# Two encoder layers on one core: the latent stage in a new order, third-attention values by features, its key heads in zero-padded tiles

## The chip, the core and the metric

The kernel runs on one core of a Trainium2 chip. That core has TensorE (PE in the profile, with its weight loads as PEld), VectorE (DVE), ScalarE (ACT), GpSimd (POOL) and the queue of SyncE (SP), which issues the transfers. The metric is the device time of one execution in microseconds (us).

## What is computed

Two layers, each on 512 tokens of 1024 features. The part that matters here is the token mixer: one projected input feeds three attentions, A (causal), C (a window of two chunks of 64 tokens, with 2 key heads for 8 query heads) and B (multi-head latent attention), in that order in the kernel.

```python
h = rms_norm(x, g_mix_pre[i])
z = h @ w_in[i]
aq, ak, av, af, bcq, bckv, bkpe, cq, ck, cv = jnp.split(z, offsets, axis=-1)
...
qf = (rms_norm(bcq, g_mla_q[i]) @ w_mla_uq[i]).reshape(b, s_len, B_HEADS, B_NOPE + B_ROPE)
q_nope, q_pe = qf[..., :B_NOPE], rope(qf[..., B_NOPE:], pos)
kvf = (rms_norm(bckv, g_mla_kv[i]) @ w_mla_ukv[i]).reshape(b, s_len, B_HEADS, B_NOPE + B_V)
k_nope, vbr = kvf[..., :B_NOPE], kvf[..., B_NOPE:]
k_pe = jnp.broadcast_to(rope(bkpe[:, :, None, :], pos), (b, s_len, B_HEADS, B_ROPE))
qb = jnp.concatenate([q_nope, q_pe], axis=-1).transpose(0, 2, 1, 3)
kb = jnp.concatenate([k_nope, k_pe], axis=-1).transpose(0, 2, 1, 3)
yb = blocked_attention(qb, kb, vbr.transpose(0, 2, 1, 3), (B_NOPE + B_ROPE) ** -0.5, False)
yc = banded_sink_attention(cq, ck, cv, sink[i], rel_bias)
...
merged = ga * (ya @ w_branch_a[i]) + gb * (yb @ w_branch_b[i]) + gc * (yc @ w_branch_c[i])
```

## The kernel before

All large products are made of three passes: weights and activations are each split into a high and a low part (`wh`/`wl`, `xnh`/`xnl`, `y0h`/`y0l`, `zkvh`/`zkvl`), and `three()` (L592) multiplies high by high, high by low and low by high. Every engine's program is written out by hand, with semaphores between them. The weights come in chunks of 128x1024 numbers, listed in `CHUNKS`, one list for all engines:

- kf, kA, qA, vA: keys' gates and the A attention's inputs. Then stage A: the chunks qC (4), kC and vC, with the 38 steps of attention A spread between their matmuls.
- Stage C: the 12 chunks gate0 and branch0, with the 38 steps of attention C (the code's attention 1; "third attention" in the title is this one of the reference's C). Its scores are L746, its transposes L756, its products with the values L768.
- The latent stage, between `ST_LAT` and `ST_B`: zq (4 chunks) and zkv (2) make the latents, then uqn (2), uqp, ukn and ukv project them up to B's queries, keys and values. No attention step stands here.
- Stage B: 12 chunks of gate1 and branch1 with the steps of attention B (scores L742), then gate2, branch2, the output product, the channel mixer and the last sub-layer.

For each chunk ScalarE copies the raw weights to `wh` (`hi`, L1007) and VectorE subtracts to make `wl` (`lo`, L1251). There are two pairs of `wh`/`wl`, so that the copy of chunk c+1 waits until TensorE is through with chunk c-1. The results go to two PSUM banks `G` in turn: a tile of results can start when the one two before it has been read out (`g_empty`). Small products (row sums, transposed scales, rotations) go through two banks `AB` in the order of the list `AUX`, in the same manner.

What each engine does in the latent stage before: VectorE scales each latent (L1492), ScalarE squares it (L1017) and makes its high part (L1096), GpSimd adds the squares (L1701, L1703), VectorE makes the low part (L1397). TensorE sums the squares over the features (L604), VectorE takes the inverse root (L1272 to L1277), and TensorE spreads it over the partitions (L620) as `rbq` and `rbkv`. VectorE alone reads out all up-projections: queries (L1403, L1404 and, for the rotary part, L1500), keys (L1403, L1404) and values (L1409); and it does the whole rotation (L1508 to L1524) after the last keys. Then ScalarE copies the shared rotary key to the 8 heads (L1100).

vC before is made by tokens: a weight of 128 columns moves against each of 4 blocks of 128 tokens. A C score takes 64 rows of the array, `kC[r:r + HD]` with `r` 0 or 64:

```python
r, k0 = HD * (h // 4), (0 if i == 0 else P * i - CH)
q, k = qC[r:r + HD, h % 4, P * i:P * i + P], kC[r:r + HD, k0:k0 + nk(i)]
```

## Time and profile before

| what | value |
|---|---|
| median of 3 runs | 2093.56 us (2093.19 to 2094.24) |
| the profiled execution's own time | 2093.33 us |
| its span in the trace | 2091.3 us |
| TensorE busy | 2009.2 us, 96% of the span |
| VectorE, ScalarE, GpSimd busy | 54%, 37%, 6% |
| mean granted TensorE clock | 0.981 of full speed |

The profiled execution lies within the spread of the timed runs, so terms read from the trace can be taken off its own time. TensorE is busy nearly always, but matmuls overlap in the trace, so their starts (one to the next) tell what each costs, and the printed duration does not. One layer's stages in the trace: A from 88 to 181 us, C to 290.9, the latent stage to 384.3, then B. The second layer repeats them some 1038 us later.

### The profile page before, as it was taken

What the parts mean: (1) busy time and instruction counts of PE and PEld (TensorE: products, weight loads), DVE (VectorE), ACT (ScalarE), POOL (GpSimd) and SP (SyncE); (2) the same over time, 40 slices, a digit from 0 to 9 for tenths busy, and PEclk for the clock granted to TensorE, in tenths of its full rate; (3) what the DMA queues carried; (4) which work ended last, traced back from release to release, by engine and by line L of the source; (5) the groups of instructions that cost most, each with busy time, mean ns of one, the idle gap of its engine ahead of it and who ended that gap; (6) DMA issues with size and microseconds to landing.
All of it is one profiled execution on the core that took longest, in us unless ns stands there. A gap on an engine that the chain in (4) does not pass through costs nothing. (4 is left out here: it accounts for less than half of the span.)

```text
span 2091.3 us, 26428 instructions
## 1 busy us (share of the span) xinstructions
PE 2009.2 (96%) x9541; PEld 1622.4 (78%) x9541; DVE 1131.8 (54%) x1983; ACT 783.3 (37%) x1359; POOL 122.6 (6%) x91
## 2 busy tenths in 40 slices
PE   8999998899999999999989999978999999999997
PEld 6777776677878888888867777757788788888886
DVE  5444446544566767525674444464445677774266
ACT  4243431343344444314433434314433344443152
POOL 0000000001100111000000000100001011010000
PEclk9999999899999999999999999989999999999999
DMA  5411132112422333332343111321124233333321
GB/s 156 106 33 41 53 85 75 40 51 61 162 81 84 97 100 93 98 121 91 86 126 81 31 51 51 91 61 51 41 78 154 81 91 100 99 92 111 104 88 71
DMA packets 256436, 176.06 MB, mean 84 GB/s; under 512 B 52148, under 2 KB 240464, under 8 KB 256080
## 3 DMA queue, kind: packets, MB, share of 16 engines
q1 hardware_dynamic: 256200, 174.56, 28.5%
q8 instruction: 63, 1.03, 0.2%
q10 hardware_dynamic: 136, 0.16, 0.1%
q14 instruction: 37, 0.30, 0.0%
HBM read 170.31 MB, written 4.36 MB: 84 GB/s over the span
## 5 line engine op out<-in xcount | busy, mean ns | idle before, releaser
L592 PE MATMUL psum<-xnh,wh 128*128 128x512 f32 (+1 forms) x1408 | 569.0, 404 | 10.0 <-DVE vB L1409 6.3
L592 PE MATMUL psum<-xnh,wl 128*128 128x512 f32 (+1 forms) x1408 | 552.4, 392 | 0.0
L592 PE MATMUL psum<-xnl,wh 128*128 128x512 f32 (+1 forms) x1408 | 551.6, 392 | 0.0
L1251 DVE TENSOR_TENSOR wl<-raw,wh 128x1024 fp32r<-128x1024 f32 (+1 forms) x276 | 364.0, 1319 | 327.2 <-ACT wh L1007 326.6
L1007 ACT ACTIVATE wh<-raw 128x1024 fp32r<-128x1024 f32 (+1 forms) x276 | 291.6, 1056 | 527.0 <-PE psum L592 518.6
L592 PEld LDWEIGHTS psum<-xnh,wh 128*128 128x128 f32 (+1 forms) x1408 | 265.8, 189 | 68.0 <-issue 17.4
L592 PEld LDWEIGHTS psum<-xnh,wl 128*128 128x128 f32 (+1 forms) x1408 | 264.8, 188 | 58.8 <-issue 0.2
L592 PEld LDWEIGHTS psum<-xnl,wh 128*128 128x128 f32 (+1 forms) x1408 | 266.0, 189 | 49.7 <-issue 0.2
L1366 DVE TENSOR_REDUCE mx<-psum 128x1 f32<-128x128 f32 (+3 forms) x128 | 62.6, 489 | 163.0 <-PE psum L743 145.4
L1061 ACT ACTIVATE Pr<-psum,nm 128x128 f32<-128x128 f32 (+3 forms) x128 | 67.7, 529 | 207.4 <-DVE nm L1367 207.4
L592 PE MATMUL psum<-wh,fh 128*128 128x512 f32 x288 | 112.0, 389 | 0.0
L592 PE MATMUL psum<-wh,fl 128*128 128x512 f32 x288 | 112.0, 389 | 0.0
L592 PE MATMUL psum<-wl,fh 128*128 128x512 f32 x288 | 112.0, 389 | 0.0
L1534 DVE TENSOR_TENSOR ub<-psum,rb 128x512 f32<-128x512 f32 x88 | 60.8, 691 | 61.2 <-PE psum L592 60.9
L1724 POOL TENSOR_TENSOR fl<-cv,fh 128x512 f32 x44 | 57.1, 1298 | 542.9 <-ACT fh L1138 542.9
L756 PE MATMUL psum<-cst,Pr 128*128 128x128 f32 x432 | 83.0, 283 | 2.7 <-DVE y0l L1389 2.7
L1073 ACT ACTIVATE PT<-psum 128x256 f32<-128x256 f32 (+3 forms) x192 | 76.5, 399 | 12.1 <-PE psum L756 12.1
L756 PEld LDWEIGHTS psum<-cst,Pr 128*128 128x128 f32 x432 | 47.3, 142 | 38.6 <-issue 26.1
L1138 ACT ACTIVATE fh<-cv 128x512 f32 (+1 forms) x44 | 27.9, 633 | 131.2 <-DVE cv L1553 131.2
L592 PE MATMUL psum<-y0h,wh 128*128 128x512 f32 x176 | 73.4, 417 | 0.0
L1476 DVE TENSOR_TENSOR th<-psum,rb 128x512 f32<-128x512 f32 x48 | 33.1, 689 | 73.0 <-PE psum L592 73.0
L592 PE MATMUL psum<-y0h,wl 128*128 128x512 f32 x176 | 70.7, 402 | 0.0
(235 smaller groups left out, 3023.8 us busy)
## 6 DMA issues: line engine op xcount, KB each, us to landing
raw<-in_w_up_dram SPq DMA_DIRECT2D x88, 512.0 KB, 3.7
raw<-in_w_gate_dram SPq DMA_DIRECT2D x48, 512.0 KB, 3.6
raw<-in_w_down_dram SPq DMA_DIRECT2D x44, 512.0 KB, 3.5
raw<-in_w_in_dram SPq DMA_DIRECT2D x40, 512.0 KB, 3.7
raw<-in_w_out_dram SPq DMA_DIRECT2D x16, 512.0 KB, 3.6
raw<-in_w_ple_gate_dram SPq DMA_DIRECT2D x16, 512.0 KB, 4.3
raw<-in_w_in_dram SPq DMA_DIRECT2D x16, 256.0 KB, 3.3
raw<-in_w_branch_a_dram SPq DMA_DIRECT2D x8, 512.0 KB, 3.3
```

The lines of the kernel that those rows point to most:

```text
L592: ins = pe.matmul(out, left, right, start=start and n == 0, stop=stop and n == 2)
L756: ins = pe.transpose(b[:, P * j:P * j + P], src[:, c0 + P * j:c0 + P * j + P], ident)
L1007: act.activation(halves(c)[0][:, 0:n], raw[s][:, 0:n], ACT.Copy).then_inc(w_hi.sem, 1)
L1061: act.activation(Pr[s % 2][:, c0:c0 + nk], src[:, 0:nk], ACT.Exp, bias=nm[:, i % 2, h:h + 1], scale=scale, accum_out=rsum[:, i % 2, h:h + ...
L1073: act.activation(PT[u % 2][:, 0:w], TBK[tbank[a][("pt", u)]][:, 0:w], ACT.Copy).then_inc(pt_ready.sem, 1)
L1138: act.activation(fh[:, bass.ds(p, 1), :], ft[pair][:, :].rearrange("p (o t) -> p o t", o=1), ACT.Copy).then_inc(f_hi.sem, 1)
L1251: dve.tensor_tensor(low[:, 0:n], raw[(L * NCH + c) % RAW][:, 0:n], hi[:, 0:n].bitcast(F32), ALU.subtract).then_inc(w_lo.sem, 1)
L1366: link(L, dve.tensor_reduce(m, b[:, 0:nk], AX_X, ALU.max))
L1476: dve.tensor_tensor(th[m % 2][:, :], b[:, :], rb[:, :], ALU.mult).then_inc(g_empty.sem, 1)
L1534: dve.tensor_tensor(u[:, 2:T + 2], G[g % 2][:, :], rb[:, :], ALU.mult).then_inc(g_empty.sem, 1)
L1724: pool.tensor_tensor(fl[:, bass.ds(p, 1), :], ft[j][:, :].rearrange("p (o t) -> p o t", o=1), fh[:, bass.ds(p, 1), :].bitcast(F32), ALU.su ...
```

## The change

- The latent stage's up-projections stand in the order uqp, uqn, uqn, ukv, ukn (before: uqn, uqn, uqp, ukn, ukv).
- The queries' inverse root is no longer spread over the partitions nor multiplied into the queries. It is kept by token (`rq`, `nrq`) and goes into the softmax of attention B, as the scale of the exponential and the factor of the maximum. ScalarE reads out the queries and the values with plain copies; VectorE keeps the keys.
- The rotation of the queries is done after uqn instead of after ukn, by VectorE in place, and ScalarE copies its result to the heads in 8 instructions. The shared key's rotation and its copy to 8 heads move up to the middle of the latents.
- VectorE adds the squares, GpSimd none. The row sums of the query latents (L604 before, L610 after) are taken after zkv 1, those of the key latents after the first uqn.
- vC comes before kC and is made by features like all others (24 matmuls of 512 columns); four transposes after kC's product turn it by tokens, and one copy puts it in place.
- kC has two tiles `kC[0]` and `kC[1]` of 128 rows, each with one head's 64 rows and zeros in the others; a score takes all 128 rows of `qC`.

The diff's pieces below are, in order: the lists, SyncE's load of the rotary table, TensorE's C score, its transposes of vC, its latent stage, ScalarE's latent stage, the softmax of attention B, VectorE's read-outs of vC and kC, and its latent stage.

```diff
-    + [("qC", m) for m in range(4)] + [("kC", 0), ("vC", 0)]
+    + [("qC", m) for m in range(4)] + [("vC", 0), ("kC", 0)]
...
-CHUNKS += [("uqn", 0), ("uqn", 1), ("uqp", 0), ("ukn", 0), ("ukv", 0)]
+CHUNKS += [("uqp", 0), ("uqn", 0), ("uqn", 1), ("ukv", 0), ("ukn", 0)]
...
-AUX = ["rb0", "vec", "csq", "rbq", "cskv", "rbkv", "rot0", "rot1", "rotk", "rb2", "pt0", "pt1"]
+AUX = ["rb0", "vec", "rotk", "csq", "cskv", "rot0", "rot1", "rbkv", "rb2", "pt0", "pt1"]
...
-                if c == ST_LAT + 5:
+                if c == ST_LAT + 4:
                     wait(y_lo.sem, y_lo.at(L, 2 * TB))
...
-                    r, k0 = HD * (h // 4), (0 if i == 0 else P * i - CH)
-                    q, k = qC[r:r + HD, h % 4, P * i:P * i + P], kC[r:r + HD, k0:k0 + nk(i)]
+                    k0 = 0 if i == 0 else P * i - CH
+                    q, k = qC[:, h % 4, P * i:P * i + P], kC[h // 4][:, k0:k0 + nk(i)]
...
+                if kind == "kC":
+                    pe.wait_ge(g_empty.sem, g_empty.at(L, G_BASE[c]))
+                    o = g_open(1)
+                    for t in range(TB):
+                        ins = pe.transpose(o[:, P * t:P * t + P], th[0][:, P * t:P * t + P], ident)
+                    ins.then_inc(vt_full.sem, 1)
...
+            slot(L, ST_LAT)
+            slot(L, ST_LAT + 1)
+            b = aux_open(L, "rotk")
+            pe.matmul(b[:, :], rot[0:ROPE, :], kf[0:ROPE, :], start=True, stop=True).then_inc(aux_full.sem, 1)
+            for c in range(ST_LAT + 2, ST_LAT + 8):
+                slot(L, c, beside=lambda k, c=c: c == ST_LAT + 5 and k == KT - 1 and z_sums(L, "q"))
+            z_sums(L, "kv")
+            turn_half(L, 0)
+            slot(L, ST_LAT + 8, beside=lambda k: turn_half(L, 1))
+            slot(L, ST_LAT + 9, beside=lambda k: spread_scale(L, "kv"))
+            slot(L, ST_LAT + 10)
...
-            for c in range(ST_LAT, ST_B):
+            for c in range(ST_LAT, ST_LAT + 6):
                 slot(L, c)
+            shared_key(L)
+            hi(L, ST_LAT + 7)
+            post(L, ST_LAT + 5)
+            queries_out(L, ST_LAT + 6, 0)
+            for c in (ST_LAT + 7, ST_LAT + 8):
+                queries_out(L, c - 1, 1)
+                hi(L, c + 1)
+                queries_out(L, c, 0)
+            queries_out(L, ST_LAT + 8, 1)
+            hi(L, ST_LAT + 10)
+            act.wait_ge(g_empty.sem, g_empty.at(L, G_BASE[ST_B - 2]))
+            for t in range(TB):
+                values_out(L, ST_B - 2, t)
+            hi(L, ST_B)
+            for j in range(2):
+                turned_queries(L, j)
...
-                scale = BSCALE if a == 2 else 1.0
+                scale = rq[:, i:i + 1] if a == 2 else 1.0
...
-                dve.tensor_scalar(neg, m, -BSCALE if a == 2 else -1.0, None, ALU.mult).then_inc(max_done.sem, 1)
+                dve.tensor_scalar(neg, m, nrq[:, i:i + 1] if a == 2 else -1.0, None, ALU.mult
+                                  ).then_inc(max_done.sem, 1)
...
+                elif kind == "vC":
+                    dve.tensor_tensor(th[0][:, :], b[:, :], rb[:, :], ALU.mult).then_inc(g_empty.sem, 1)
+                    for g in range(2):
+                        dve.memset(kC[g][HD - HD * g:P - HD * g, :], 0.0)
...
+            elif kind == "kC":
+                dve.wait_ge(w_used.sem, w_used.at(L, c + 1))
+                for g in range(2):
+                    own = slice(HD * g, HD * g + HD)
+                    ins = dve.tensor_tensor(kC[g][own, :], G[G_BASE[c] % 2][own, :], rb[own, :], ALU.mult)
+                ins.then_inc(g_empty.sem, 1)
+                dve.wait_ge(vt_full.sem, vt_full.at(L, 1))
+                dve.tensor_copy(vC[:, :, :].rearrange("p t e -> p (t e)"), G[(G_BASE[c] + 1) % 2]
+                                ).then_inc(g_empty.sem, 1)
...
                 j = c - ST_LAT - 2
-                if 0 <= j < 6 and j != 5:
+                if 0 <= j < 6:
                     latent_lo(L, j)
-                if j == 3:
+                    add_squares(L, j)
+                if j == 2:
+                    shared_key(L)
+                if j == 4:
                     row_scales(L, "q")
-                if j == 4:
-                    latent_lo(L, 5)
-                    scale_rows(L, "q", rbq)
+                if j == 6:
                     row_scales(L, "kv")
-                if j == 5:
-                    scale_rows(L, "kv", rbkv)
+                    rope(L, 0)
+                    rope(L, 1)
```

What stands in each engine's row, at three places. First ScalarE in the latent stage of layer 0, from the read-out of the second-last latent on, before the change. L1007 is the copy of a weight chunk, L1017 a square, L1096 a latent's high part.

```order
L1007 ACTIVATE wh<-raw 128x1024 [waits w_landed2,w_used]
L1017 ACTIVATE sq_82<-Sp_72 128x512 [waits sq_used,g_empty]
L1096 ACTIVATE zkvh<-Sp_72,vec 128x512
L1007 ACTIVATE wh<-raw 128x1024 [waits w_landed3,w_used]
L1007 ACTIVATE wh<-raw 128x1024 [waits w_landed0,w_used]
L1007 ACTIVATE wh<-raw 128x1024 [waits w_landed1,w_used]
L1007 ACTIVATE wh<-raw 128x1024 [waits w_landed2,w_used]
L1100 ACTIVATE kB<-ytok 32x4096 [waits kpe_ready]
L1007 ACTIVATE wh<-raw 128x1024 [waits w_landed3,w_used]
```

And the same engine and place of the changed kernel (L1012 is the copy of a weight chunk there, L1019 a square, L1100 a high part):

```order
L1148 ACTIVATE kB<-ytok 32x4096 [waits kpe_ready]
L1012 ACTIVATE wh<-raw 128x1024 [waits w_landed2,w_used]
L1019 ACTIVATE sq_82<-Sp_72 128x512 [waits sq_added,g_empty]
L1100 ACTIVATE zkvh<-Sp_72,vec 128x512
L1133 ACTIVATE Pr_73<-psum 128x512 [waits t_full,g_full]
L1133 ACTIVATE Pr_74<-psum 128x512 [waits t_full,w_used]
L1012 ACTIVATE wh<-raw 128x1024 [waits w_landed3,w_used]
L1136 ACTIVATE qB<-psum 64x512 [waits g_full]
L1137 ACTIVATE qB<-psum 64x512
...
L1142 ACTIVATE vB<-psum,rcol 128x512 [waits rcol_ready,w_used]
L1012 ACTIVATE wh<-raw 128x1024 [waits w_landed2,w_used]
L1155 ACTIVATE qB<-Pr_73 32x512 [waits rope_sum]
```

The copy of the shared key (32x4096) stands ahead of the weight chunks of the up-projections instead of behind them, and the read-outs of queries, values and rotated queries stand between the weight copies.

Second, VectorE at the end of the latent stage, before the change (keys' third and fourth tile, the rotation, the first values):

```order
L1403 TENSOR_TENSOR kB<-psum,rbkv 64x512 [waits w_used]
L1404 TENSOR_TENSOR kB<-psum,rbkv 64x512
L1508 TENSOR_TENSOR Pr_73<-Sp_71,trig 128x512 [waits trig_in]
L1511 TENSOR_TENSOR PT_75<-psum,trig 128x512 [waits aux_full]
L1514 TENSOR_TENSOR qB<-Pr_73,PT_75 32x512 [waits aux_empty]
L1514 TENSOR_TENSOR qB<-Pr_73,PT_75 32x512 x3
L1508 TENSOR_TENSOR Pr_74<-Sp_72,trig 128x512
L1511 TENSOR_TENSOR PT_76<-psum,trig 128x512 [waits aux_full]
L1514 TENSOR_TENSOR qB<-Pr_74,PT_76 32x512 [waits aux_empty]
L1514 TENSOR_TENSOR qB<-Pr_74,PT_76 32x512 x3
L1518 TENSOR_TENSOR th_77<-kf,trig 32x512
L1521 TENSOR_TENSOR th_78<-psum,trig 32x512 [waits aux_full]
```

And after it (L1305 is the low part of a weight chunk there, L1472 and L1473 the keys):

```order
L1573 TENSOR_TENSOR Pr_74<-Pr_74,PT_76 128x512 [waits aux_empty,dve_link]
L1305 TENSOR_TENSOR wl<-raw,wh 128x1024 [waits w_hi]
L1363 COPY rbkv<-psum 128x512 [waits aux_full]
L1472 TENSOR_TENSOR kB<-psum,rbkv 64x512 [waits g_full,g_empty,aux_empty]
L1473 TENSOR_TENSOR kB<-psum,rbkv 64x512
L1472 TENSOR_TENSOR kB<-psum,rbkv 64x512 [waits g_full]
L1473 TENSOR_TENSOR kB<-psum,rbkv 64x512
L1305 TENSOR_TENSOR wl<-raw,wh 128x1024 [waits w_hi]
L1472 TENSOR_TENSOR kB<-psum,rbkv 64x512 [waits g_full]
L1473 TENSOR_TENSOR kB<-psum,rbkv 64x512
L1472 TENSOR_TENSOR kB<-psum,rbkv 64x512 [waits w_used]
L1473 TENSOR_TENSOR kB<-psum,rbkv 64x512
```

The rotation is gone from behind the keys; the keys are the stage's last read-out, with the low part of gate1's first chunk between the second and the third tile.

Third, TensorE at the border of stages A and C in the changed kernel (L791 are the last transposes of attention A, L838 the four of vC, L760 the first score of attention C):

```order
L791 MATMUL psum<-cst,ytok 128x128 x3
L598 MATMUL psum<-xnh,wh 128x512
L598 MATMUL psum<-xnl,wh 128x512
L598 MATMUL psum<-xnh,wl 128x512
L598 MATMUL psum<-xnh,wh 128x512
L598 MATMUL psum<-xnl,wh 128x512
L598 MATMUL psum<-xnh,wl 128x512
L838 MATMUL psum<-cst,th_77 128x128 [waits g_empty]
L838 MATMUL psum<-cst,th_77 128x128 x3
L598 MATMUL psum<-xnh,wh 128x512 [waits g_empty,w_lo,w_hi]
L598 MATMUL psum<-xnl,wh 128x512
L598 MATMUL psum<-xnh,wl 128x512
```

Before, 24 matmuls of vC (128x128, with no attention among them) stood between those last transposes and the first chunk of stage C, and that chunk's bank had been read out long before; now six matmuls of kC and the four transposes stand there, and the first chunk of stage C waits (`g_empty`) for the read-out of kC's tile.

## Rows read from the trace of the kernel before

**Rows 1.** Page, part 1: busy time, share of the span, instructions.

```profile
PE 2009.2 (96%) x9541; PEld 1622.4 (78%) x9541; DVE 1131.8 (54%) x1983; ACT 783.3 (37%) x1359; POOL 122.6 (6%) x91
```

**Rows 2.** Waits of PE: for what, us in total, times, longest.

```profile
PE psum L592 <- DVE vB L1409: 11.9, 4, 3.2
...
PE psum L924 <- DVE PT L1511: 10.0, 2, 5.0
PE psum L592 <- DVE Sp L1500: 6.4, 2, 3.2
PE psum L604 <- POOL acc L1701: 6.4, 2, 3.2
```

**Rows 3.** Windows: length, busy us of each engine, granted clock, DMA share, GB/s.

```profile
290.85:384.30 93.45, 76.17 (x296) 58.92 (x294) 57.29 (x88) 23.15 (x25) 7.06 (x4) 0.88 0.27 68
384.30:390.10 5.80, 5.80 (x17) 4.71 (x18) 1.24 (x5) 0.46 (x2) 0.00 (x0) 0.50 0.27 90
```

**Rows 4.** Timeline of PE, latent stage of layer 0: start, us, instruction.

```profile
290.85 0.39 PE L592 MATMUL psum<-xnh,wh 128*128 128x512 f32 x1
...
317.82 0.39 PE L592 MATMUL psum<-xnh,wl 128*128 128x512 f32 x1
318.05 0.95 PE L604 MATMUL psum<-cst,acc 128*128 128x1 f32 x8
...
360.14 1.88 PE L922 MATMUL psum<-Sp,cst 128*128 128x512 f32 x4
367.00 2.07 PE L924 MATMUL psum<-kf,cst 32*128 32x512 f32 x2 [4.98 <-DVE PT L1511]
...
384.29 0.76 PE L592 MATMUL psum<-xnh,wh 128*128 128x512 f32 x1 [3.16 <-DVE vB L1409]
```

**Rows 5.** Timeline of PE, chunk vC of layer 0, a stretch without attention.

```profile
175.07 0.28 PE L592 MATMUL psum<-wl,xnh 128*128 128x128 f32 x1
...
177.75 0.28 PE L592 MATMUL psum<-wl,xnh 128*128 128x128 f32 x1
```

**Rows 6.** Timeline of PE around an A score (65 rows), then a C score (64).

```profile
94.69 0.40 PE L592 MATMUL psum<-xnh,wl 128*128 128x512 f32 x1
94.92 0.38 PE L742 MATMUL psum<-kA,qA 65*128 65x128 f32 x2
95.15 0.22 PE L743 MATMUL psum<-cbf 128*128 128x128 bf16 x1
...
236.03 0.39 PE L592 MATMUL psum<-xnh,wl 128*128 128x512 f32 x1
236.35 0.59 PE L746 MATMUL psum<-kC,qC 64*128 64x192 f32 x2
236.87 0.44 PE L756 MATMUL psum<-cst,Pr 128*128 128x128 f32 x2
```

**Rows 7.** Timelines of ACT and DVE, last tile of attention A.

```profile
178.52 0.60 ACT L1079 ACTIVATE y0h<-psum 128x512 fp32r<-128x512 f32 x1 [6.90 <-PE psum L777]
179.15 0.69 DVE L1389 TENSOR_TENSOR y0l<-psum,y0h 128x512 fp32r<-128x512 f32 x1 [4.19 <-ACT y0h L1079]
```

**Rows 8.** Groups by form, whole trace: busy us, mean ns, idle before.

```profile
L1007 ACT ACTIVATE wh<-raw 128x1024 fp32r<-128x1024 f32 x274 | 290.6, 1061 | 523.6 <-PE psum L592 518.6 <-DMA raw<-in_w_up_dram 2.4 <-DMA raw<-in_w_ple_dram 1.9
...
L1117 ACT ACTIVATE pl<-psum 128x512 f32<-128x512 f32 x16 | 9.3, 596 | 7.9 <-PE psum L592 7.8
...
L1100 ACT ACTIVATE kB<-ytok 32x4096 f32<-32x4096 f32 x2 | 7.2, 3615 | 29.1 <-DVE ytok L1524 29.1
...
L1251 DVE TENSOR_TENSOR wl<-raw,wh 128x1024 fp32r<-128x1024 f32 x274 | 363.0, 1325 | 325.1 <-ACT wh L1007 324.5
...
L1397 DVE SCALAR_TENSOR_TENSOR y0l<-Sp,vec,y0h 128x512 fp32r<-128x512 f32 x8 | 12.1, 1518 | 0.0
...
L1403 DVE TENSOR_TENSOR kB<-psum,rbkv 64x512 f32<-64x512 f32 x8 | 5.5, 683 | 5.5 <-PE psum L592 5.3
...
L1701 POOL TENSOR_TENSOR acc<-sq,sq 128x512 f32<-128x512 f32 x4 | 6.9, 1727 | 586.6 <-ACT sq L1017 586.6
```

More of the change, by code:

```diff
@@ L106 @@
 WIDTH = {"kf": KT * 40}
-G_OF = {"vA": 0, "out": 0, "down": 0, "pg": 0, "vC": 2, "uqn": 2, "uqp": 2, "ukn": 4, "ukv": 4, "ple": TB,
+G_OF = {"vA": 0, "out": 0, "down": 0, "pg": 0, "kC": 2, "uqn": 2, "uqp": 2, "ukn": 4, "ukv": 4, "ple": TB,
         "branch0": 2, "branch1": 2, "branch2": 2}
@@ L338, in trunk_kernel @@
     trig = here("trig", 48, [P, 2, T])
-    rbq = here("rbq", 52, [P, T])
     rbkv = here("rbkv", 54, [P, T])
@@ L829, in slot @@
                             ins.then_inc(wide_full.sem, 1)
-            elif kind == "vC":
-                for j in range(2):
-                    o = g_open(j)
-                    for t in range(2):
-                        tb = 2 * j + t
-                        for k in range(KT):
-                            ins = three(o[:, P * t:P * t + P], c, P * k, P, xnh[:, k, P * tb:P * tb + P],
-                                        xnl[:, k, P * tb:P * tb + P], k == 0, k == KT - 1, w_moves=True)
-                            if t == 1 and k == KT - 1:
-                                ins.then_inc((w_used if j == 1 else g_full).sem, 1)
-                            if k % 4 == 3:
-                                between(4 * j + 2 * t + k // 4)
             elif kind[:6] == "branch":
@@ L858, in slot @@
                     ins.then_inc((w_used if j == 1 else g_full).sem, 1)
+                    if j == 0 and beside is not None:
+                        beside(0)
             elif kind == "ukn":
@@ L872, in slot @@
                     ins.then_inc((w_used if t == TB - 1 else g_full).sem, 1)
+                    if t == 1 and beside is not None:
+                        beside(0)
             elif kind == "ple":
@@ L1118, in ple_out, with taken_bank, queries_out, values_out @@
                                ).then_inc(g_empty.sem, 1)
+        def taken_bank(L, c, j):
+            if j == G_OF[CHUNKS[c][0]] - 1:
+                act.wait_ge(w_used.sem, w_used.at(L, c + 1))
+            else:
+                act.wait_ge(g_full.sem, g_full.at(L, GP_BASE[c] + j + 1))
+            return G[(G_BASE[c] + j) % 2]
+        def queries_out(L, c, j):
+            kind, m = CHUNKS[c]
+            b = taken_bank(L, c, j)
+            if kind == "uqp":
+                act.wait_ge(t_full.sem, t_full.at(L, 2 * STEPS))
+                act.activation(Pr[j][:, :], b, ACT.Copy).then_inc(g_empty.sem, 1)
+            else:
+                h = 4 * m + 2 * j
+                act.activation(qB[0:HD, h, :], b[0:HD, :], ACT.Copy)
+                act.activation(qB[0:HD, h + 1, :], b[HD:P, :], ACT.Copy).then_inc(g_empty.sem, 1)
+        def values_out(L, c, t):
+            b = taken_bank(L, c, t)
+            act.wait_ge(rcol_ready.sem, rcol_ready.at(L, RB_NORMS.index("kv") + 1))
+            act.activation(vB[:, t, :], b, ACT.Copy, scale=rcol[:, t:t + 1]).then_inc(g_empty.sem, 1)
+        def shared_key(L):
+            if L > 0:
+                act.wait_ge(x_spilled.sem, 16 * L)
+            act.wait_ge(kpe_ready.sem, kpe_ready.at(L, 1))
+            act.activation(kB[NOPE:NOPE + ROPE, :, :],
+                           ytok[0:ROPE, :].rearrange("p (o t) -> p o t", o=1).to_broadcast([ROPE, H, T]),
+                           ACT.Copy).then_inc(kpe_placed.sem, 1)
+        def turned_queries(L, j):
+            act.wait_ge(rope_sum.sem, rope_sum.at(L, j + 1))
+            for q in range(4):
+                ins = act.activation(qB[NOPE:NOPE + ROPE, 4 * j + q, :], Pr[j][32 * q:32 * q + 32, :], ACT.Copy)
+            ins.then_inc(rope_ready.sem, 1)
         def up_post(L, s, it):
@@ L1399, in latent_lo, with add_squares @@
                                      ).then_inc(z_lo.sem, 1)
+        def add_squares(L, j):
+            if j in (0, 4):
+                return
+            dve.wait_ge(sq_ready.sem, sq_ready.at(L, j + 1))
+            if j in (2, 3):
+                dve.wait_ge(sq_added.sem, sq_added.at(L, j - 1))
+            out, one = (sq[0], sq[0]) if j == 5 else (acc, sq[0] if j == 1 else acc)
+            dve.tensor_tensor(out[:, :], one[:, :], sq[j % 2][:, :], ALU.add).then_inc(sq_added.sem, 1)
         def heads_apart(L, b, dst, j, scale):
@@ L1463, in post @@
                                       ).then_inc(wide_empty.sem, 1)
[L1464 to L1470 removed]
+            elif kind == "kC":
[7 more added lines that the diff above has]
+                                ).then_inc(g_empty.sem, 1)
             elif kind[:4] == "gate":
                 br = int(kind[4])
+                if br == 1 and m == 0:
+                    dve.wait_ge(g_empty.sem, g_empty.at(L, G_BASE[c]))
                 if br == 2 or (br == 1 and m >= 2):
@@ L1557, in slot @@
             last = CHUNKS[c - 1][0] if c else None
-            late = last not in ("ukn", "ukv") and kind not in ("ukn", "ukv")
-            if not late:
-                lo(L, c + 1)
             if last == "ukn":
```

183 lines of the change are left out of this document (65 added, 118 removed).

## Prediction

> **What bounds the kernel now.** First the busy shares: TensorE is busy 2009.2 of 2091.3 us, VectorE 54%, ScalarE 37% [rows 1]. So time can come from TensorE's own work or from its few waits, from nothing else. Next TensorE's waits: the four longest groups, 11.9, 10.0, 6.4 and 6.4 us, all fall in the latent stage [rows 2], the same ones in each layer, 34.7 us together or 17.3 a layer. In three the one waited for is VectorE's read-out or rotation, in the fourth GpSimd's addition. The windows then show a second price of these waits: over the 93.45 us of layer 0's latent stage the granted clock is 0.88 of full, and in the 5.80 us behind its last wait it is 0.50, which is 1.2 instead of 2.4 GHz [rows 3]. Since a share of 1 - 0.88 lost means twice that share at the lower level, some 22 us of the stage ran there.
>
> **Latent stage, what can be had.** At the full clock 119 steps from matmul to matmul take 317.82 - 290.85 = 26.97 us, 0.2266 each [rows 4]. The stage has 11 chunks of 24: 264 x 0.2266 = 59.8 us. Its small products: two row sums at 0.8 (318.05 to the next start, close to the printed 0.95), four rotation matmuls in 1.7 to 1.9, the shared key's, 2.07 at the low clock, so 1.0 to 1.1, two spreads of some 0.35, and about 0.1 at each of nine returns to the large products: 6 us [rows 4]; the last two figures are estimates. So 66 us of work stand in a stage of 384.29 - 290.85 = 93.4 [rows 4]: 27.4 us are waits and low clock. Behind it 5.8 us at half clock hold 2.7 us more [rows 3]. At most 30 us a layer.
>
> **What the new order leaves of it.** I count from the first zq as 0, with 5.44 us a chunk. The changed rows put uqp at 34.6, uqn at 40 and 47 to 54, ukv at 54 to 59 and ukn last. ScalarE's queue is the one to follow, as a late weight copy stops TensorE. A weight copy costs 1.06, a read-out of 128x512 0.6, the shared key's copy 3.62 [rows 8]. Zkv 0 is squared and copied by 31; the key's copy, now ahead of everything, runs 31 to 34.7; the copy for the first uqn ends at 35.8, VectorE's low part (1.33 [rows 8]) at 37.1, needed at 40. Behind it queue the second zkv's square (added on VectorE at 44.5, wanted at 45.5 by the row sum, the thinnest margin) and the read-outs of uqp (38.1, 40.8). Each later chunk costs ScalarE 1.06 + four half read-outs of 0.6 = 3.5 of 5.44 us. It fits: low parts are done at 43, 49 and 57, wanted at 47, 54 and 59.5. The values wait for rcol, ready at 52. The rotation is on VectorE from 51.7 to 56, while TensorE runs uqn and ukv, so the 4.98 us wait of the shared key's matmul [rows 4] has nothing left to wait for: that matmul moved to where `kf` is long ready. Removing `rbq` takes a spread (0.35) and VectorE's copy away. In the queue of SyncE the rotary table moves one weight chunk up, behind a wait for attention C's last low part; that falls near the start of zq 0, and the next weight load cannot go before zq 1's low part anyway: nothing.
>
> What is late next are keys. Two read-outs of 64 rows, 0.68 each [rows 8], serve one tile that TensorE makes in 6 x 0.2266 = 1.36: VectorE only just keeps up, it begins when the last values are out (60.4), and the low part of gate1's chunk stands between tile 2 and tile 3. I get a wait of 0.3 in ukv, 0.35 before ukn's third tile and 1.25 before gate1, whose bank is ukn's third: 1.9 a layer. Whether a wait as short as 1.3 us drops the clock is open; a drop cost 2.7 us behind the stage's last wait of 3.2 [rows 3, 4], and I take a third of that, 0.8. Latent stage: 27.4 + 2.7 + 0.35 - 1.9 - 0.8 = **27.7 us a layer**.
>
> On VectorE four additions of 0.7 are new, but its low parts of the latents took 1.52 us in the mean [rows 8], and ran beside GpSimd's additions of 1.73 [rows 8]. The Trainium skill, VectorE: DVE Perf Modes, writes of the second SBUF read interface as shared with GpSimd; by that the low parts fall back to about the 0.7 of a read-out and pay for the additions. By the sum above VectorE had room either way.
>
> **vC by features.** 24 matmuls of 128x128 take 177.75 - 175.07 = 2.68 us, 0.112 each [rows 5]; 96 are 10.7 us. After: 24 x 0.2266 = 5.4, four transposes 0.45 (as 128x128 matmuls), and about 0.05 more at each of some eight switches between attention and 512 columns, 0.4. **4.4 us a layer**, all on TensorE's path. The attention steps are the same and have waited for nothing there.
>
> **Padded key heads.** An A score (65 rows, so no half of the array) begins 94.92 - 94.69 = 0.23 behind the last product, and the next instruction begins 0.23 behind it, for 128 columns in two passes; 192 columns are 0.34. A C score (64 rows, 192 columns) begins 0.32 behind and lasts 0.52 to the next start [rows 6]. So 0.84 against 0.57: 0.27 for each; with 128 columns likewise. 32 scores a layer: **8.8 us a layer**. The Trainium skill, TensorEngine Tiling (Array Packing), Key Properties, says that a change of tiling mode drains TensorE, and here the gap ahead of the 64-row score agrees. The same section speaks against the padding too: 64-row tiles work independently, two scores at once. By the drain the sum is 17.6 us for both layers, by lost overlap it would be nothing. In [rows 6] each 64-row score stands alone among 128-row products, so no overlap is there to lose; the streamed columns are the same.
>
> **Border of stages A and C.** New here: the last transposes of attention A stand 6 matmuls before kC's end. ScalarE's copy begins 178.52 and VectorE's low part 179.15 to 179.84 [rows 7], some 2.0 us behind the transposes; counted from kC's end, at +0.2 or so. Only then come kC's two read-outs, 2 x 0.68, and gate0 waits for them: +1.75, against +0.46 when TensorE is through with vC's transposes. A wait of 1.3 us, plus 0.4 for the smaller chance of a low clock: **-1.7 us a layer**. The copy of vC (0.7) and the 3 first matmuls of gate0 (0.7) then run side by side.
>
> Sum: 27.7 + 4.4 + 8.8 - 1.7 = 39.2 a layer, **78.4 us**. The profiled execution's own time of 2093.33 is 0.2 below the median, so both give 2093.3 - 78.4 = **2015 us**.
>
> **Bounds.** Below: no new wait, no low clock, 45 a layer: 2003. The unmeasured things: the scores' saving, 0.20 to 0.33 each (13 to 21 us); ScalarE's half read-outs from PSUM, 0.6 by the nearest row, at most 1.06, that of twice the columns [rows 8]; the exponential with a scale per token, which by its neighbours costs nothing or up to 0.1 for 64 steps, hidden; and the low clock, 0 to 5.4 us a layer. With all of them bad at once the gain is still 78 - 5 - 9 - 8 = 56, that is 2037.
>
> **Rivals.**
> 1. ScalarE's queue is late in the latent stage. For it: 32x4096 (3.62) now blocks weight copies, and the row sum of the keys has 1 us of margin. Against: ScalarE was busy 23.15 of 93.45 us there [rows 3], and 22 added copies of 0.6 make 36 of 66. If each of three or four chunks waits 1.5 us and the clock falls each time, 10 us a layer are given back: 2035. Chance 0.13.
> 2. Padding does nothing, the gap belongs to fp32 behind the split products. Against: the A score has no such gap [rows 6]. 2033. Chance 0.05.
> 3. It is slower. One mechanism: the read-outs on ScalarE. The latent stage has 22 new ScalarE instructions a layer, each between a weight copy and the bank TensorE waits for. They cost 0.6; if they cost 1.8 us more each, all in TensorE's way, 39.6 us a layer are gone and the time is 2094; from there on it is slower, at 2.5 more each it is 2125. Only the 3.62 of the 4096-column copy is of that size, and it has eight times the columns. Chance 0.04, a quarter of it within 0.2% of no change.
> 4. The order takes the waits away, but short ones keep the clock low: two more drops a layer of 2.7 us, 2026. Chance 0.14, inside the range.
> The forecast itself: 0.64.
>
> A measurement of this kernel can tell 0.2%, 4 us. All cases but the third are faster: faster 0.96, same 0.01, slower 0.03. Range: from 2005, near the bound, to 2037, past rivals 1 and 2.
>
> **What the profile will show.** TensorE's waits in the latent stage 1 to 3 us a layer, none on a rotation, none on GpSimd; the stage some 67 us long at a granted clock near 1. C scores 0.23 behind their predecessor and 0.34 to the next. vC's chunk with 512 columns, a wait near 1.3 at gate0's first matmul with VectorE's kC as releaser, and one like it at gate1. Wrong would be: waits for ScalarE's copies (`wh`, `qB`, `vB`) of over 5 us a layer, or a granted clock under 0.95 there.

## The result, and the profile after

The changed kernel takes 2011.32 us in the median of 4 runs (2010.56 to 2016.67) against 2093.38 of the kernel before beside it: the ratio is 0.9615, 95% interval 0.9601 to 0.9629, faster by 82.1 us (by the interval 78 to 84). The forecast was 2015 (2005 to 2037). The profiled execution took 2011.93, its span is 2010.1 us. One execution of e2_vc below took 2144.42 us at a granted clock of 0.898 and is left out of its median.

First the busy shares of the changed kernel, page part 1, which answer to [rows 1]:

```profile
span 2010.1 us, 26179 instructions
PE 1954.9 (97%) x9397; PEld 1599.2 (80%) x9397; DVE 1106.0 (55%) x1955; ACT 815.2 (41%) x1403; POOL 107.6 (5%) x83
```

ScalarE has taken work over (783.3 us before), and VectorE is busy 26 us less: its read-outs went, and the squares' additions that came are small. Waits of TensorE (for whom, us in total, times, the longest), against [rows 2]; the first, for `xt`, is outside of all that was changed:

```profile
PE psum L644 <- DVE xt L1394: 11.4, 4, 4.4
...
PE psum L770 <- DVE y0l L1448: 2.7, 2, 1.4
PE psum L598 <- DVE kB L1473: 2.7, 4, 1.1
PE psum L598 <- DVE kC L1535: 2.3, 2, 1.1
```

The four groups of the latent stage, 34.7 us, are gone; `kB` and `kC` (2.7 and 2.3 us in both layers) are the forecast's new waits at gate1 and gate0, and nothing of the rotation or of GpSimd is left. Windows of the changed kernel: from the first zq to B's first score in layer 0, the 5.80 us behind it, stages A and C of layer 0, then stage C and the latent stage of layer 1 (length in us, busy us of each engine, granted clock, DMA share, GB/s), against [rows 3]:

```profile
277.02:345.12 68.10, 66.77 (x295) 52.96 (x293) 40.11 (x72) 36.55 (x47) 0.00 (x0) 1.00 0.35 87
345.12:350.92 5.80, 5.80 (x32) 4.90 (x31) 3.20 (x8) 1.56 (x8) 0.00 (x0) 1.00 0.47 140
89.07:177.08 88.01, 84.00 (x500) 66.75 (x501) 39.39 (x93) 39.76 (x108) 0.00 (x0) 1.00 0.13 37
177.08:277.02 99.94, 97.34 (x534) 82.51 (x534) 49.54 (x147) 43.15 (x123) 0.00 (x0) 1.00 0.23 65
1174.50:1274.41 99.91, 97.38 (x534) 82.41 (x534) 49.61 (x147) 43.11 (x123) 0.00 (x0) 1.00 0.23 65
1274.41:1342.51 68.10, 66.77 (x294) 52.95 (x293) 40.12 (x72) 36.56 (x47) 0.00 (x0) 1.00 0.36 88
```

The granted clock of the stage was 0.88 before and is 1.00 now; in the stretch behind it it went from 0.50 to 1.00. From the first zq to B's first score it is 68.10 us in both layers, 94.85 and 94.58 before. Between the same marks (the first scores of A, C and B, the first zq, the first matmul of the output product) the two traces give, layer 0 and layer 1:

| stretch | before | after | gain |
|---|---|---|---|
| A score to C score | 92.89, 91.25 | 88.01, 88.06 | 4.9, 3.2 |
| C score to zq | 109.03, 109.04 | 99.94, 99.91 | 9.1, 9.1 |
| zq to B score | 94.85, 94.58 | 68.10, 68.10 | 26.8, 26.5 |
| B score to output product | 183.58, 183.40 | 182.10, 182.09 | 1.5, 1.3 |

They sum to 82.3; with 1.1 lost elsewhere, nearly all behind the last output product, that is 81.2, the difference of the spans. The 1.6 by which layer 0's first row exceeds layer 1's is a stretch of low clock that, of these two executions, only the one of the kernel before has there. It comes and goes (see the fourth experiment), so it is no gain of the change.

At the border of A and C, timeline of PE of the changed kernel (start, duration, instruction, wait); the C scores answer to the 64-row score in [rows 6]:

```profile
176.31 0.47 PE L598 MATMUL psum<-xnh,wh 128*128 128x512 f32 x1 [1.14 <-DVE kC L1535]
176.62 0.39 PE L598 MATMUL psum<-xnl,wh 128*128 128x512 f32 x1
176.85 0.40 PE L598 MATMUL psum<-xnh,wl 128*128 128x512 f32 x1
177.08 0.39 PE L760 MATMUL psum<-kC,qC 128*128 128x128 f32 x2
177.22 0.48 PE L598 MATMUL psum<-xnh,wh 128*128 128x512 f32 x1
```

A score begins 0.23 behind its predecessor, where it was 0.32 to 0.35. Over all 64 scores of each trace, from the start of the predecessor to the start of what follows the score, it was 0.84 to 0.85 with 192 columns and 0.75 with 128, and is 0.55 and 0.45 now: 0.3 less for a score, 0.1 ahead of it and 0.2 behind. The heads in rows 0 to 63 and those in rows 64 to 127 were alike before. Groups by form of the changed kernel, the copies that went to ScalarE and two that stayed (busy us, mean ns, idle before), against [rows 8]:

```profile
L1148 ACT ACTIVATE kB<-ytok 32x4096 f32<-32x4096 f32 x2 | 7.3, 3628 | 0.0
...
L1456 DVE SCALAR_TENSOR_TENSOR y0l<-Sp,vec,y0h 128x512 fp32r<-128x512 f32 x8 | 6.0, 746 | 0.0
...
L1142 ACT ACTIVATE vB<-psum,rcol 128x512 f32<-128x512 f32 x8 | 5.5, 689 | 3.8 <-PE psum L598 3.6
...
L1137 ACT ACTIVATE qB<-psum 64x512 f32<-64x512 f32 x8 | 4.8, 595 | 0.1
L1136 ACT ACTIVATE qB<-psum 64x512 f32<-64x512 f32 x8 | 4.7, 592 | 15.0 <-PE psum L598 15.0
```

The half read-outs cost the 0.6 that was taken for them. The low parts of the latents fell from the 1518 ns of [rows 8] to 746 (why: fourth experiment).

### The profile page after: what moved, and what is told of

The parts are those of the page before. It is cut to its first block, busy times and chain, and to the rows that moved or that the text cites. A ratio compares the mean times of both kernels' runs of the same rounds, so it can differ in the third digit from the quotient of the medians.

```text
span 2010.1 us, 26179 instructions
## 1 busy us (share of the span) xinstructions
PE 1954.9 (97%) x9397; PEld 1599.2 (80%) x9397; DVE 1106.0 (55%) x1955; ACT 815.2 (41%) x1403; POOL 107.6 (5%) x83
## 4 chain that ended last, share of the span: by engine, by line
PE 88%; DVE 6%; issue 3%; ACT 3%; DMA 0%; SPq 0%; DVEq 0%; ACTq 0%
PE psum L598 76%; PE psum L782 4%; PE psum L756 3%; PE psum L770 2%; ACT wh L1012 1%; PE psum L760 1%; DVE xt L1394 1%; PE psum L644 1%; DVE mx L1424 1%; PE psum L791 1%; DVE yg_down L1386 0%; DVE oP L1375 0%; ACT Pr L1065 0%; ACT PT L1077 0%; DVE xnl L1319 0%
## 5 line engine op out<-in xcount | busy, mean ns | idle before, releaser
L1305 DVE TENSOR_TENSOR wl<-raw,wh 128x1024 fp32r<-128x1024 f32 (+1 forms) x276 | 364.4, 1320 | 318.6 <-ACT wh L1012 318.0
L1012 ACT ACTIVATE wh<-raw 128x1024 fp32r<-128x1024 f32 (+1 forms) x276 | 291.2, 1055 | 452.8 <-PE psum L598 444.7
L1754 POOL TENSOR_TENSOR merged<-merged,th 128x512 f32<-128x512 f32 x32 | 43.1, 1351 | 976.1 <-DVE th L1556 975.8
L1065 ACT ACTIVATE Pr<-psum,nm,rq 128x128 f32<-128x128 f32 (+3 forms) x64 | 39.6, 619 | 108.9 <-DVE nm L1425 108.9
L1176 ACT ACTIVATE fh<-cv 128x512 f32 (+1 forms) x44 | 27.8, 632 | 131.3 <-DVE cv L1613 131.3
L770 PEld LDWEIGHTS psum<-cst,Pr 128*128 128x128 f32 x432 | 51.0, 142 | 27.7 <-issue 15.3
```

Source lines behind the costliest of these rows:

```text
L770: ins = pe.transpose(b[:, P * j:P * j + P], src[:, c0 + P * j:c0 + P * j + P], ident)
L1012: act.activation(halves(c)[0][:, 0:n], raw[s][:, 0:n], ACT.Copy).then_inc(w_hi.sem, 1)
L1065: act.activation(Pr[s % 2][:, c0:c0 + nk], src[:, 0:nk], ACT.Exp, bias=nm[:, i % 2, h:h + 1], scale=scale, accum_out=rsum[:, i % 2, h:h + ...
L1305: dve.tensor_tensor(low[:, 0:n], raw[(L * NCH + c) % RAW][:, 0:n], hi[:, 0:n].bitcast(F32), ALU.subtract).then_inc(w_lo.sem, 1)
L1754: pool.tensor_tensor(merged[:, m, :], merged[:, m, :], th[m % 2][:, :], ALU.add).then_inc(m_added.sem, 1)
```

## Experiments: the parts by themselves

The code cuts below are shortened: they show what changes, not every line. Four kernels ran on one chip beside the kernel before, which took 2091.69 there.

**e1_pad**, the kernel before with the padded heads alone (the score is shown; kC's two fills and two read-outs come with it):

```diff
-r, k0 = HD * (h // 4), (0 if i == 0 else P * i - CH)
-q, k = qC[r:r + HD, h % 4, P * i:P * i + P], kC[r:r + HD, k0:k0 + nk(i)]
+k0 = 0 if i == 0 else P * i - CH
+q, k = qC[:, h % 4, P * i:P * i + P], kC[h // 4][:, k0:k0 + nk(i)]
```

> The kernel before with one part of the change: the key heads of attention C in two zero-padded tiles of 128 rows. Theory (a 64-row score among 128-row products makes TensorE stop and start again): each of the 64 scores gains 0.27 to 0.29 us, so 17 to 18.5 us, 2075 to 2076; the score starts 0.23 behind the product before it. Rival (the gap belongs to fp32 products behind the split ones, whatever their rows): no gain, 2093. VectorE's two fills and second read-out, 1.7 us a layer, lie beside products of vC and cost nothing under either.

Measured: 2072.71, ratio 0.9915 (0.9903 to 0.9928), -19.0 us. Stage C from its first score to zq fell from 109.03 (what TensorE was busy in it: 107.15) to the first line here; the second is the same stage of the kernel with vC alone. Windows:

```profile
180.10:280.60 100.50, 97.50 (x534) 82.61 (x534) 49.71 (x147) 43.52 (x124) 0.00 (x0) 1.00 0.22 64
```
```profile
178.40:287.43 109.03, 107.15 (x535) 79.22 (x535) 49.37 (x147) 43.14 (x123) 0.00 (x0) 1.00 0.20 58
```

At the same number of matmuls and the same clock it is 8.5 us a layer less, 0.27 for each of 32 scores. That is net of new waits: the third score starts 0.77 behind its predecessor, 0.37 of it idle for the first exponential, and TensorE waits three times 0.16 for ScalarE's `PT`. By the starts, as above, a score with half of the rows between products with all of them costs 0.3 more, though it streams the same columns.

**e2_vc**, the kernel before with vC by features ahead of kC, transposed behind it (the lists and the read-out; one `kC` as before):

```diff
-[("kC", 0), ("vC", 0)]
+[("vC", 0), ("kC", 0)]
+ins = pe.transpose(o[:, P * t:P * t + P], th[0][:, P * t:P * t + P], ident)
```

> The kernel before with one part of the change: vC by features, kC last, with kC in one tile of 64-row heads as before. Theory: 4.4 us a layer less of TensorE's work, less a wait for kC's read-out at gate0 of about 0.5 (one read-out of 0.69 instead of two), so 3.9 a layer, 2085.5. Rival (the added wait also drops the clock, 2.7 us each time): 2088 to 2091.

Measured: 2081.34, ratio 0.9951 (0.9938 to 0.9964), -10.4. In its trace the stretch from A score to C score is 89.03 and 89.07, in both layers with one stretch of low clock of 1.6: without it 3.8 a layer less than before, 7.6 in all, which lies at the lower end of the interval. With one read-out of kC the wait at gate0 is 0.4, and no low clock stands behind it: the rival did not come.

**e3_latent**, the changed kernel with vC and the key heads as before (the diff's pieces on `vC`, `kC` and the C score undone):

> The changed kernel with vC by tokens and the key heads of attention C in one tile, as before, so that only the latent stage and the softmax scale of attention B differ from before. Theory: 27.7 us a layer by the forecast's sum, 2038; TensorE waits 1 to 2 us a layer there and its clock is full. Rival (part of the gain comes from elsewhere, such as an earlier start of attention B's steps or fewer low-clock stretches at other places): 2045 or more.

Measured: 2039.44, ratio 0.975 (0.9737 to 0.9762), -52.3; zq to B score is 68.10, what the changed kernel has. The forecast's 27.7 a layer would be 55.4. In the trace the last two stretches of the table give 56.0, and 2.8 are lost from the output products on, where one low stretch is 3.4 us longer than in the trace before. So the three parts give 19.0 + 10.4 + 52.3 = 81.7 by themselves and 82.1 together: within the 3 us that each interval allows, they do not overlap.

**e4_pool_squares**, the changed kernel with the squares added by GpSimd, at the moved places:

```diff
-add_squares(L, j)   # VectorE, behind each latent's low part
+for j in (1, 2, 3, 5):   # GpSimd
+    add_squares(L, j)
```

> The changed kernel with the squares of the latents added on GpSimd again, all else as changed. Theory (it is the later place of the row sums that took the wait away, not the engine): GpSimd's four additions of 1.7 us end before the sums are asked for, except the last, wanted 1 us after VectorE's was ready, so at most 1 us of wait a layer: 2011 to 2014. Rival (the engine made the wait): 3.2 us of wait and 2.7 of low clock a layer come back, 2023.

Measured: 2014.19, ratio 0.9627 (0.9615 to 0.964). TensorE waits for no row sum, and zq to B score is 68.10 and 68.11: the later place is enough to take the wait away, whichever engine adds. Two groups of its trace, then VectorE and GpSimd at one latent:

```profile
L1456 DVE SCALAR_TENSOR_TENSOR y0l<-Sp,vec,y0h 128x512 fp32r<-128x512 f32 x8 | 12.2, 1520 | 0.0
L1745 POOL TENSOR_TENSOR acc<-acc,sq 128x512 f32<-128x512 f32 x4 | 7.2, 1808 | 17.1 <-ACT sq L1019 17.1
```
```profile
303.32 1.23 DVE L1305 TENSOR_TENSOR wl<-raw,wh 128x1024 fp32r<-128x1024 f32 x1 [0.34 <-ACT wh L1012]
303.88 1.81 POOL L1745 TENSOR_TENSOR acc<-acc,sq 128x512 f32<-128x512 f32 x1 [3.63 <-ACT sq L1019]
304.47 1.77 DVE L1456 SCALAR_TENSOR_TENSOR y0l<-Sp,vec,y0h 128x512 fp32r<-128x512 f32 x1
```

The mean of 1520 ns mixes two values, here as in [rows 8]: the low parts with an addition beside them take 1.77 to 1.78 us, those with none 0.75. So the low part and the addition together cost VectorE less by itself (some 1.4 us) than the low part alone does beside GpSimd. The low part shown ends 0.55 behind the addition that was running when it began. The Trainium skill, VectorE: DVE Perf Modes, Two Vector instructions with no wait between them, was drawn on for this in the prediction (a read interface shared with GpSimd); the trace agrees, 1.78 against 0.75 us, now by switching it.

Its median lies 2.9 us above the changed kernel's, its profiled execution (2016.48) 4.6, and none of it is in the latent stage. Of the 4.6, 3.2 are low clock in stage A of both layers: a window of e4_pool_squares, and the same of the changed kernel:

```profile
117.10:120.50 3.40, 3.40 (x14) 2.75 (x13) 0.58 (x2) 0.75 (x4) 0.00 (x0) 0.50 0.33 98
```
```profile
117.10:120.50 3.40, 3.40 (x19) 2.62 (x18) 0.58 (x2) 0.96 (x4) 0.00 (x0) 1.00 0.24 71
```

Both stand behind the same wait, which every kernel of this study has once a layer; here it is in the changed one:

```profile
115.83 0.44 PE L770 MATMUL psum<-cst,Pr 128*128 128x128 f32 x2 [1.38 <-DVE y0l L1448]
```

In the 14 profiled executions of this study the wait was 1.37 or 1.38 us 28 times, and 12 times a 3.4 us stretch at half clock stood behind it, which costs 1.6. That is up to 3.2 us of the 2 to 6 us by which each kernel's runs differ. The other runs have no trace, but their time goes with the clock: of the changed kernel's four, the fastest (2010.56) was granted 0.995 and the slowest (2016.67) 0.992. This makes a gain of 2 us hard to see below.

## Experiments: who is the bound, and what a wait costs

Four kernels on a second chip (the kernel before: 2091.35), then four on a third (2093.09).

**e5_dve_queries**, uqn's read-outs back on VectorE:

```diff
-act.activation(qB[0:HD, h, :], b[0:HD, :], ACT.Copy)   # and the other half
+dve.tensor_copy(qB[0:HD, h, :], b[0:HD, :])   # and the other half, in VectorE's row
```

> The changed kernel, with one thing back: the eight 64-row read-outs of uqn's queries a layer are VectorE's again, as plain copies, instead of ScalarE's (uqp's and the values' stay with ScalarE). Theory, the order made the gain and VectorE has room: a chunk of uqn costs VectorE 1.33 for its low part and 4 x 0.68 for the read-outs, 4.05 of the 5.44 us that TensorE takes, so the time is that of the changed kernel within 0.2%, 2009 to 2016 us, with at most a few tenths of new wait in the latent stage. Rival, the relief of VectorE made it: its queue (latents' low parts, squares, rotation, rbkv, keys) is late by some 5.4 us a layer at the end of the stage, the rotation and the keys come late, waits of 2 to 5 us a layer appear with low clock behind them: 2018 to 2030 us.

Measured: 2023.36, ratio 0.9668 (0.9654 to 0.9681). My theory fell, and the rival's size is right: some 12 us, though its waits for keys and rotation did not come. The timeline of PE:

```profile
332.90 0.39 PE L598 MATMUL psum<-y0h,wl 128*128 128x512 f32 x1
335.37 0.70 PE L598 MATMUL psum<-wh,zkvh 128*128 128x512 f32 x1 [2.08 <-DVE qB L1569]
```

and of DVE, before that wait ends:

```profile
327.73 0.16 DVE L1341 TENSOR_SCALAR rtmp<-psum 128x4 f32<-128x4 f32 x1
...
329.99 0.68 DVE L1576 TENSOR_TENSOR PT<-psum,trig 128x512 f32<-128x512 f32 x1
...
333.23 0.69 DVE L1579 TENSOR_TENSOR Pr<-Pr,PT 128x512 f32<-128x512 f32 x1
333.84 0.68 DVE L1568 COPY qB<-psum 64x512 f32<-64x512 f32 x1
```

The inverse root of the keys' scale and the rotation, 6.1 us together, stand ahead of the second chunk's read-outs. zq to B score is 71.81 in both layers, 3.7 more: 2.08 of wait and 1.6 of low clock behind it. That makes 7.4 in both layers; its profiled execution has stage A's low clock in both as well, 3.2.

**e10_late_rotation**, the same with the rotation behind those read-outs:

```diff
-if j == 6: row_scales(L, "kv"); rope(L, 0); rope(L, 1)
+if j == 6: row_scales(L, "kv")
+if j == 7: rope(L, 0); rope(L, 1)
```

> As the run with uqn's read-outs on VectorE, but with the rotation of the queries one chunk later there, behind the read-outs of the second uqn chunk. Theory, what cost 7 us was the place and not the load: the row scales and the rotation (6 us) stood ahead of two read-outs for which TensorE waited 2.1 us a layer, with low clock behind; with them out of the way the waits for qB go and the time is that of the changed kernel or up to 2 us more, 2010 to 2014. Rival, VectorE has too much work there whatever its order: a wait of 1 us or more a layer comes back at the keys or at ukv (for the rotated queries or rbkv), and it stays at 2018 to 2023.

Measured: 2015.42, ratio 0.9636 (0.9622 to 0.9649). Of the wait for `qB` 0.12 is left, and zq to B score is 68.70. The 0.6 more than in the changed kernel are 0.2 at the values' tile behind that wait and 0.4 at `rbkv`'s spread, which waits 0.20 for the rotation. The profiled execution took 2012.98, inside what was expected; the median is 1.4 above that and 3.1 above the changed kernel's on the same chip, where the two intervals still overlap. So VectorE can carry these read-outs at 0.6 us a layer, and e5 lost its time by their place; putting them on ScalarE only spared the change from having to place them well.

**e6_gap3** and **e7_gap6**, the changed kernel with a longer wait ahead of gate0 (n = 3 and 6):

```diff
 elif kind == "kC":
     dve.wait_ge(w_used.sem, w_used.at(L, c + 1))
+    for _ in range(n):
+        link(L, dve.memset(vC[:, :, :], 0.0))
```

> The changed kernel with three more fills of vC with zeros on VectorE, each waiting for the one before, ahead of kC's read-outs (nothing that is computed changes). They lengthen TensorE's wait ahead of gate0 from 1.1 to about 2.7 us. Theory, a wait of this length drops the clock (all waits of 2.7 us and more did in the kernel before, those of 1.1 never did in the changed one): 1.6 of wait and about half of a 3.4 us stretch at half clock, 1.7, a layer, 6 to 7 us in all: 2017 to 2019. Rival, the clock falls only with longer waits: 3 us, 2014 to 2015, and no stretch below full clock behind gate0's start.

> As the one before with six fills, so that TensorE waits about 4.3 us ahead of gate0. Theory: the wait is 3.2 us a layer longer than in the changed kernel and the stretch at half clock costs 1.7 or, as behind the waits of 3.2 to 6 us in the kernel before, 2.7 to 3.4: 10 to 13 us in all, 2021 to 2025. Rival, a drop doesn't depend on this wait: 6.4 us, 2018.

Measured: 2020.56 and 2026.45, ratios 0.9668 and 0.9687, against 2011.80 of e8_pool_lo on the same chip, which ties with the changed kernel (next experiment). The waits were longer than meant, one PE line of each:

```profile
178.68 0.77 PE L598 MATMUL psum<-xnh,wh 128*128 128x512 f32 x1 [3.11 <-DVE kC L1537]
```
```profile
1185.95 0.76 PE L598 MATMUL psum<-xnh,wh 128*128 128x512 f32 x1 [5.09 <-DVE kC L1537]
```

and a stretch of low clock came with each of the four. Windows of e6 in layer 0, then of e7 in layer 1:

```profile
177.70:184.50 6.80, 5.82 (x16) 4.80 (x17) 4.96 (x14) 0.52 (x3) 0.00 (x0) 0.50 0.24 77
```
```profile
1183.00:1189.80 6.80, 3.85 (x10) 3.20 (x11) 5.76 (x12) 0.00 (x0) 0.00 (x0) 0.50 0.11 24
```

From A score to zq, with the added wait (1.97 and 3.95) and any low clock of stage A taken off, the stretch cost 2.56 and 1.41 in e6 (6.8 and 3.4 us long) and 1.42 and 1.57 in e7 (3.4 and 6.8). In these four cases a wait that is 2 us longer does not cost more in low clock: of e7's 6.8 us, 2.95 ran off while TensorE still waited. The theory that the drop comes with these waits holds; that it would grow with the wait does not. From one fill to the next it took 0.66 us instead of the 0.53 assumed, so both times lie above what was expected: 3.9 + 4.0 for e6 and 7.9 + 3.0 for e7 by these sums, against the measured 8.8 and 14.7; of the latter 1.6 is stage A's low clock in the profiled execution, and some 2.3 lie far from the wait: 0.85 ahead of A's first score, 0.5 and 0.95 behind the two output products.

**e8_pool_lo** and **e11_pool_lo_again**, gate1's first low part on GpSimd:

```diff
+if c == ST_B:
+    dve.wait_ge(w_lo.sem, w_lo.at(L, ST_B + 1))
+if c + 1 != ST_B:
     lo(L, c + 1)
# GpSimd makes that low part
+pool.tensor_tensor(wl, raw, wh, ALU.subtract).then_inc(w_lo.sem, 1)
```

> The changed kernel, but the low part of gate1's first weight chunk is made by GpSimd instead of VectorE, where it stands between the keys' second and third tile. Theory, this low part (1.33 us on VectorE) is what TensorE's wait of 1.1 us ahead of gate1 comes from: the wait goes, 1.1 to 1.4 us a layer, 2009 us, if GpSimd's 128x1024 subtraction (twice the 1.73 us of its 128x512 additions, some 3.5) is done before TensorE wants it about 5 us after the copy. Rival, GpSimd takes longer than that or slows VectorE's key read-outs beside it: a wait of 1 to 3 us for GpSimd in its place, 2011 to 2018.

> The changed kernel once more, to stand beside the three others on one chip. 2009 to 2013 us; a stretch at half clock in stage A, behind the 1.38 us wait for y0l, may stand in one layer or none, 1.6 us each.

> The run with gate1's first low part on GpSimd once more, beside the changed kernel on one chip. Theory: its stage is 0.97 us a layer shorter as before, and it is 2 us faster than the changed kernel in the median; what hid this was low clock in stage A of its profiled execution, which comes and goes. Rival: the low clock is moved and not removed, and the two times agree within 0.5 us.

Measured: 2011.80, ratio 0.9622 (0.9609 to 0.9635); on the third chip 2012.07 (0.962, 0.9605 to 0.9634) beside 2012.34 of the changed kernel itself (e9_changed_again: 0.9624, 0.9609 to 0.9639; there the change is worth 80.8 us). GpSimd's subtraction:

```profile
L1756 POOL TENSOR_TENSOR wl<-raw,wh 128x1024 fp32r<-128x1024 f32 x2 | 4.8, 2389 | 640.5 <-ACT wh L1012 640.5
```

takes 2.39, not 3.5, and the key read-outs beside it keep their 683 and 693 ns. The wait of 1.11 at gate1 is gone, and zq to B score is 67.13 and 67.13 in the one, 67.14 and 67.15 in the other, 0.96 a layer less. The time does not show it: the medians on one chip agree within 0.3 us, as the rival of e11 had it and not its theory. Low clock in stage A stands in one layer of each of their profiled executions and in none of e9's, and the last stretch, from the second output product to the end, is 485.9 and 486.3 us against 485.5 and 484.5 in the changed kernel's two executions. Whether the 1.9 us are hidden by chance or given back by the clock, 5 runs with a spread of 2.3 to 6.2 us cannot say.

**e12_gate_bank**, the same, and the transposes of vC go to a bank of the scores:

```diff
-o = g_open(1)
+o = SB[1]
 for t in range(TB):
     ins = pe.transpose(o[:, P * t:P * t + P], th[0][:, P * t:P * t + P], ident)
```

> As the run with gate1's first low part on GpSimd, and the transposes of vC go to a bank of the scores (free by then) instead of the second result bank. So gate0 has the bank that vC's product left long ago, and no longer waits for kC's two read-outs; attention C's first score does, about 0.9 us later. Theory: the wait of 1.1 us ahead of gate0 shrinks to some 0.3 ahead of the score, 0.7 to 0.8 a layer, 1.5 us faster than the kernel it is made from: 2007 to 2009. Rival: the wait only moves to the first score and stays 1 us long, no change.

Measured: 2011.57, ratio 0.9616 (0.9603 to 0.9629), no change against e11's 2012.07. Gate0 waits no more, but PE's timeline has two waits in its place:

```profile
178.24 0.49 PE L763 MATMUL psum<-kC,qC 128*128 128x128 f32 x2 [0.35 <-DVE kC L1539]
...
183.07 0.49 PE L763 MATMUL psum<-kC,qC 128*128 128x128 f32 x2 [0.66 <-ACT Pr L1068]
```

0.35 + 0.66 = 1.01 of 1.14, and A score to zq is 187.94 in layer 1, where the changed kernel has 187.97. The rival held in size, and the place is new: the third score of C reuses the first one's bank and waits for its exponential, which comes late because VectorE at the border does kC, vC, a low part and the fills of `biasC` and `Pr` before its first softmax (one behind the other from 176.79 to 181.71 us in this trace, the softmax at 181.94). VectorE's row bounds the border; the wait at gate0 was only where that showed first.

## Why the prediction was right, and its terms

**Latent stage, 27.7 a layer.** Measured 28.2 and 27.8 (the last two rows of the table). Its base, that 66 of 93.4 us are work, is near: 68.10 less the 0.77 from gate1's start to the score is 67.33, of which 1.3 are waits, so 66.0 is left, where 65.65 was due without `rbq`'s spread. ScalarE's row went as worked out: the shared key's copy ran from 30.9 to 34.5 us behind the first zq (forecast 31 to 34.7), and the keys' squares were added 1.2 us ahead of their sum. The waits were set too high: 1.9 against the measured 1.33 (0.22 and 1.11, forecast 0.35 and 1.25, and the 0.3 in ukv didn't come), and the 0.8 for a clock drop was not due. These two would have made 29.1. What took it back: 0.3 and 0.6 in the stage's work and base, and the 5.8 us at half clock behind it, priced at 2.7, gave 2.1 and 1.9 (gate1's start to the output product: 184.99 and 184.81 before, 182.87 now). That the term came within 0.5 us is in part luck, two errors that cancelled.

**Short waits and the clock (rival 4, 0.14).** It did not happen. The waits of 1.10 to 1.14 us at gate0 and gate1 were followed by no low clock in any of the 30 cases of these traces; those of 1.38 were in 12 of 28, those of 2.08 in e5 and of 3.1 and 5.1 in e6 and e7 in all 6, one of e1_pad's two of 2.13, and every one of 2.6 and more in the 14 traces, but for the 3.8 to 4.1 us at each execution's very start. Length alone does not decide: the wait of 1.48 to 1.50 for `ytok` at the end of stage C was never followed by low clock, in 28 cases. The charge of 0.8 + 0.4 a layer was for a risk that these two waits did not carry.

**Padded scores, 8.8.** (32 x 0.27 is 8.6.) By themselves 8.5 a layer, 9.1 in the changed kernel. Each score gained 0.3, a little more than the 0.27 forecast, and short new waits took some back: 0.5 at e1_pad's third score (0.05 in the changed kernel, where gate0's wait runs while VectorE catches up), and one to three of 0.16 a layer for `PT`. Rival 2 is refuted. On the sentence of the Trainium skill, TensorEngine Tiling (Array Packing), Key Properties, that a change of tiling mode drains TensorE: e1 agrees, by 0.1 us ahead of a score and 0.2 behind it, and no lost overlap showed. That a drain is the cause is the page's word; the runs show the price of the 64 rows.

**vC 4.4, border -1.7.** Sum 2.7, measured 3.2. The wait at gate0 was 1.14 for the 1.3 forecast, and the 0.4 for the clock was not due; vC with its 0.4 of wait gave 3.8 in e2. Since e12 shows that this wait costs nothing by itself, the term -1.3 was right in size and wrong in kind: the same time is due at the third score if not here.

**Rivals 1 and 3, ScalarE.** Refuted by the 592 to 595 ns of its read-outs, and by TensorE's waits in that stage, which are for `kB` alone. e5 shows that the danger was on the other engine: what TensorE waits for is decided by what stands ahead of a read-out, and less by the load. The prediction's sentence that VectorE had room either way holds only with the right order.

**The reading of the waits.** The prediction calls 11.9, 10.0, 6.4 and 6.4 us the four longest groups, all in the latent stage. They are not: the second longest was `xt`'s, 11.4 us, all behind the output product, and it is as long now. No term used it, so the slip cost the forecast nothing.

**The sum.** The forecast was 39.2 a layer; measured were 28.0 + 9.1 + 3.2 = 40.3, each part within 0.5. The forecast's 78.4 us lies inside the interval of the measured 82.1, and on the third chip the same kernel gave 80.8, so the 3.7 between them are not clear of the noise.

## What to carry to other kernels

Sum the work between two marks at the full clock, and take it off the stretch: what is left is waits and the low clock that they bring, and both go when the waits go. When work moves to another engine to relieve a queue, ask first whether another order in the old queue does it too, and what stands directly ahead of each read-out that TensorE waits for. A wait that stands first in a stage may be only the front of a late engine: removing it there (e12) moves it to the first and the third score.
